# An ffn gain moved into the gather's copies, one more down chunk loaded ahead, and a start without the wait for constants

## The reference

```
h = _rms_norm(x, norm_mix[l]);  z = h @ w_in[l]
... three attentions of z, concatenated to mix ...
x = x + mix @ w_out[l]
x = x + _hier_moe(_rms_norm(x, norm_ffn[l]), w_group[l], b_group[l], w_expert[l], ...)
```

```
h = jax.nn.silu(xb @ w_gate[e]) * (xb @ w_up[e])
return h @ w_down[e]
```

## Time and profile before

| | |
|---|---|
| median of 3 runs | 1176.25 us (1175.04 to 1177.41) |
| the profiled execution | 1173.85 us, of which its span is 1171.9 us |
| PE busy | 930.9 us, 79% of the span |
| PE weight loads | 582.0 us, 50% |
| DVE busy | 335.0 us, 29% |
| ACT busy | 195.2 us, 17% |
| HBM read | 443.57 MB, 379 GB/s over the span |
| mean granted PE clock | 0.906 of full speed |

### The profile page before, as it was taken

One profiled execution on the slowest core, in us unless ns is written; L12 is line 12 of the kernel. 1 busy time (PEld: TensorE's weight loads), 2 busy tenths in 40 slices (PEclk: granted clock), 3 DMA queues, 4 the chain that ended last, 5 costly groups with the idle time before them and its releaser, 6 DMA issues.

```text
span 1171.9 us, 23254 instructions
## 1 busy us (share of the span) xinstructions
PE 930.9 (79%) x10294; PEld 582.0 (50%) x10299; DVE 335.0 (29%) x978; ACT 195.2 (17%) x527; POOL 18.7 (2%) x38
## 2 busy tenths in 40 slices
PE   8999999767567766775899999997776677557765
PEld 5876666434334433543478766664343434234433
DVE  3656552211111111111137465521111111111112
ACT  2234321001000100110112442211010001001002
POOL 1000000000000000000010001000000000000000
PEclk9999999989888888888999999999887888788878
DMA  7956499999999999999998256999999999999995
GB/s 308 404 237 258 200 379 423 435 428 428 427 433 426 429 426 435 425 429 427 401 386 322 80 218 270 382 429 430 427 430 427 429 426 431 428 430 427 428 424 245
DMA packets 34455, 446.16 MB, mean 381 GB/s; under 512 B 9648, under 2 KB 11056, under 8 KB 14256
## 3 DMA queue, kind: packets, MB, share of 16 engines
q1 hardware_dynamic: 33792, 444.54, 90.3%
q10 hardware_dynamic: 560, 0.09, 0.0%
HBM read 443.57 MB, written 1.05 MB: 379 GB/s over the span
## 4 chain that ended last, share of the span: by engine, by line
DMA 50%; PE 45%; issue 2%; DVE 1%; ACT 1%; another core or an unknown queue 0%; SPq 0%; ACTq 0%; POOLq 0%; POOL 0%; DVEq 0%
DMA ring<-in_w_down 18%; DMA arena<-in_gate_up 14%; DMA xb<-in_w_down 14%; PE pv L1751 10%; PE pj L1374 8%; PE tr L1776 5%; DMA ring<-in_gate_up 3%; PE pj L1380 2%; PE tr L1735 2%; PE pj L1486 2%; PE pj L1786 2%; PE pj L1606 2%; PE pj L1581 1%; PE pj L1615 1%; PE lg L1404 1%
## 5 line engine op out<-in xcount | busy, mean ns | idle before, releaser
L1751 PE MATMUL pv<-ring,xT 128*32 128x256 f32 x3072 | 228.5, 458 | 110.8 <-DMA ring<-in_gate_up 110.8
L1751 PEld LDWEIGHTS pv<-ring,xT 128*32 128x32 f32 x3072 | 110.2, 127 | 218.0 <-DMA ring<-in_gate_up 109.8
L1222 DVE TENSOR_SCALAR arena<-arena 128x128 f32<-128x128 f32 x64 | 14.5, 227 | 667.2 <-ACT arena L806 666.9
L1751 PE MATMUL pv<-arena,xT 128*32 128x256 f32 x1024 | 85.5, 500 | 67.1 <-DMA arena<-in_gate_up 67.1
L642 ACT ACTIVATE arena<-pv 128x256 f32<-128x256 f32 x64 | 24.6, 384 | 513.3 <-PE pv L1751 513.3
L1374 PE MATMUL pj<-xT,ring 128*128 128x256 f32 x448 | 100.2, 381 | 0.0
L1776 PE MATMUL tr<-ring,arena 128*32 128x256 f32 x1360 | 81.9, 380 | 16.5 <-issue 10.1
L1751 PEld LDWEIGHTS pv<-arena,xT 128*32 128x32 f32 x1024 | 38.7, 139 | 112.6 <-DMA arena<-in_gate_up 73.4
L1374 PEld LDWEIGHTS pj<-xT,ring 128*128 128x128 f32 x448 | 84.3, 190 | 12.9 <-issue 1.1
L1786 PE MATMUL pj<-arena 32*128 32x256 f32 x512 | 72.5, 400 | 6.7 <-ACT arena L642 6.7
L1786 PE MATMUL lg<-arena 32*128 32x256 f32 x512 | 72.5, 401 | 0.0
(11 more groups left out here) (237 smaller groups left out, 856.8 us busy)
## 6 DMA issues: line engine op xcount, KB each, us to landing
ring<-in_gate_up SPq DMA_DIRECT2D x42, 4096.0 KB, 48.5
ring<-in_w_down SPq DMA_DIRECT2D x38, 2048.0 KB, 41.4
arena<-in_gate_up SPq DMA_DIRECT2D x14, 4096.0 KB, 41.9
xb<-in_w_down SPq DMA_DIRECT2D x18, 2048.0 KB, 40.8
ring<-in_w_in_chunks SPq DMA_DIRECT2D x10, 2048.0 KB, 21.3
ring<-in_gate_up SPq DMA_DIRECT2D x10, 2048.0 KB, 8.2
ring<-in_w_out_halves SPq DMA_DIRECT2D x4, 2048.0 KB, 33.2
arena<-in_gate_up SPq DMA_DIRECT2D x4, 2048.0 KB, 49.4
```

Source lines behind the costliest of these rows:

```text
L1751: ins = mm(gu_ps[i * CAP:(i + 1) * CAP, :], xg[:, j, c:c + CAP], w, start=(j == 0), stop=(j == KD - 1), tile_position=(0, i * CAP), skip_g ...
```

## The change

There are three edits.

1. The weight of the ffn norm leaves `rows`. `rows` is now x times rms, copied by ACT straight from x. The weight is the per-partition scale of the copies out of the gather, for a feature lies on one partition there. A scale is one number for each partition, so one copy serves one block of 128 columns: a gather has eight copies of 128 where it had two of 512, and `gate_up` waits for each block ahead of its step. `weight`, `gain_ffn`, its two 512 KB loads and the semaphore `x_weighted` are gone.
2. The memory and the place in SP's list that `gain_ffn` had now serve the fourth chunk of down 3. The load of that chunk behind `d_used[0]` is gone.
3. PE's and DVE's waits for `consts_in` move behind the first products: DVE waits ahead of the first `diag`, PE in `spread_rms`.

```diff
-D_LOADS = {1: 2, 2: 2}
+D_LOADS = {1: 2, 2: 2, GU_PLACES - 1: 0}
...
                 sp.wait_ge(lg_done, at(l, NS, 8))
-                sp.dma_start(gain_ffn, bcast_row(norm_ffn, l, D_MODEL)).then_inc(gain_f_in, 16)
+                sp.dma_start(spare[3], down[SPLIT][:, 3]).then_inc(spare_full[3], 16)
...
                 sp.wait_ge(sums_open, l + 1)
-                sp.wait_ge(x_weighted, at(l, TOK, TOK))
+                sp.wait_ge(rows_ready, at(l, 2 * TOK, 2 * TOK))
...
-                        elif kind == "d" and e >= SPLIT:
+                        elif kind == "d" and e > SPLIT:
...
-                                ks = slice(len(spare) if e == SPLIT else 0, KE)
-                                sp.dma_start(d_place[i][:, ks], rows_of[:, ks]).then_inc(d_full[i], 16)
+                                sp.dma_start(d_place[i], rows_of).then_inc(d_full[i], 16)
...
-            act.dma_start(gain_R, ffn_blocks_d.rearrange("p (l j) -> p l j", l=DEPTH)).then_inc(gain_r_in, 16)
+            act.dma_start(gains, ffn_blocks_d.rearrange("p (u l j) -> p u l j", u=2, l=DEPTH)).then_inc(gain_r_in, 16)
...
-                    act.wait_ge(x_weighted, at(l, TOK, t + 1))
+                    act.wait_ge(x_added, at(l, PARTS, (2, PARTS)[t]))
...
-                             weighted[:, 512 * half:512 * half + 512].rearrange("q (p j) -> q p j", j=KD),
+                             x[:, t, 512 * half:512 * half + 512].rearrange("q (p j) -> q p j", j=KD),
...
                     def gathered(q):
 
-                        for half in range(2):
-                            act.wait_ge(wide_done, at(r, WIDE, gather_use(q) + half))
-                            copy(xg[:, 4 * half:4 * half + 4, :].rearrange("p j s -> p (j s)"), tr[:, half]).then_inc(wide_read, 1)
+                        for j in range(KD):
+                            if j % 4 == 0:
+                                act.wait_ge(wide_done, at(r, WIDE, gather_use(q) + j // 4))
+                            copy(xg[:, j, :], wide_ps[:, j * P:(j + 1) * P], scale=gain_G[:, l, j:j + 1]).then_inc(wide_read, 1)
...
-            dve.wait_ge(consts_in, 16)
 
             for l in range(DEPTH):
...
+                dve.wait_ge(consts_in, 16)
                 for t in range(TOK):
...
-                dve.wait_ge(ssq_ready, rbase + 6)
-                weight(0, 0, D_MODEL).then_inc(x_weighted, 1)
...
-                dve.wait_ge(rows_ready, at(l, 2 * TOK, 2))
-                own.mark(weight(1, 512, D_MODEL))
...
-                weight(1, 0, 512).then_inc(x_weighted, 1)
...
-                if l == 0:
-                    pe.wait_ge(consts_in, 16)
-
...
                 def spread_rms():
 
+                    pe.wait_ge(consts_in, 16)
                     pe.wait_ge(more_consts_in, 16)
...
-                        if j == KD // 2 and other_half:
-                            pe.wait_ge(wide_read, other_half)
+                        if gathered is not None:
+                            pe.wait_ge(wide_read, gathered + j)
```

More of the change, by code:

```diff
@@ L314, in trunk @@
         h_rows = take(HALF)
-        y = take(D_MODEL)[:, 0:D_MODEL // QUAD]
+        y = take(D_MODEL // QUAD)
         xnT_up = zT_flat[:, 1024:2048].rearrange("p (t j s) -> p t j s", t=TOK, j=KD // 2)
@@ L326, in trunk @@
         cnt = take(N_EXPERTS)
-        flags = take(N_EXPERTS * MORE)
+        flags = lam_in.rearrange("p v d -> p (v d)")[:, 0:N_EXPERTS * MORE]
         codes = take(OVER)
-        assert taken[0] <= 2048 + D_MODEL
-        taken[0] = 2048 + D_MODEL
+        assert taken[0] <= 2048
+        taken[0] = 2048
         rlog = take(TOK * R_COLS).rearrange("p (t n) -> p t n", t=TOK)
@@ L363, in trunk @@
         over_free = sem("over_free")
-        x_weighted, sums_open, rows_ready = sem("x_weighted"), sem("sums_open"), sem("rows_ready")
+        sums_open, rows_ready = sem("sums_open"), sem("rows_ready")
         sums_zeroed, upper_spent, upper_in = sem("sums_zeroed"), sem("upper_spent"), sem("upper_in")
@@ L717, in _ @@
                 square_sums(l)
+                act.wait_ge(gain_r_in, 16)
                 for t in range(TOK):
@@ L843, in _ @@
                                 act.wait_ge(o_wide, i * 2 + 1)
-                                copy(xg[:, :, 0:CAP], wide_ps[:, 0:KD * CAP].rearrange("p (j s) -> p j s", j=KD)
-                                     ).then_inc(o_wide_read, 1)
+                                for j in range(KD):
+                                    ins = copy(xg[:, j, 0:CAP], wide_ps[:, j * CAP:(j + 1) * CAP], scale=gain_G[:, l, j:j + 1])
+                                ins.then_inc(o_wide_read, 1)
                                 act.wait_ge(o_gu, i + 1)
@@ L1739, in gather, with gate_up @@
                     return last
-                def gate_up(both, c, other_half=0, signal=False, in_pieces=False):
+                def gate_up(both, c, gathered=None, signal=False, in_pieces=False):
                     for j in range(KD):
@@ L1806, in down_landed @@
                             pe.wait_ge(d_full[n % D_PLACES], d_loads(l, n))
-                        steps = [d_place[n % D_PLACES][:, k] for k in range(KE)]
                         if n == SPLIT:
@@ L1810, in down_landed @@
                                 pe.wait_ge(part_in, 16 * (l + 1))
-                            return [*spare, *steps[len(spare):]]
-                        return steps
+                            return spare
+                        return [d_place[n % D_PLACES][:, k] for k in range(KE)]
                     def tokens(q):
@@ L1914 @@
 WIDE = 2 * 2 + BODY
+READS = 2 * KD + BODY
 PAIRS = 4
@@ L1970 @@
     arrays["const_table"] = layer_constants()
-    arrays["ffn_blocks"] = np.ascontiguousarray(
-        given["norm_ffn"].reshape(DEPTH, KD, P).transpose(2, 0, 1).reshape(P, DEPTH * KD))
+    blocks = given["norm_ffn"].reshape(DEPTH, KD, P).transpose(2, 0, 1).reshape(P, DEPTH * KD)
+    steps = given["norm_ffn"].reshape(DEPTH, P, KD).transpose(1, 0, 2).reshape(P, DEPTH * KD)
+    arrays["ffn_blocks"] = np.concatenate([blocks, steps], 1)
     arrays["x_turned"] = np.ascontiguousarray(given["x"].reshape(TOK, P, P, KD).transpose(0, 2, 3, 1).reshape(TOK, P, D_MODEL))
```

31 lines of the change are left out of this document (15 added, 16 removed).

## The result

The changed kernel takes 1168.62 us (median of 5 runs, 1168.1 to 1170.0). The kernel before took 1175.04 us beside it (5 runs, 1174.32 to 1177.41). The ratio is 0.9947, with a 95% interval of 0.9934 to 0.996. That is 6.2 us less, 4.7 to 7.8. The forecast was 1171.0 us, 5.2 us less than before.

What follows compares the result with a forecast made beforehand. The prediction took the expert load stream at 429 GB/s as the bound. Bytes 2.44, SP's list 2.28 and the start 0.5 make 5.2 us, off the median of 1176.25: 1171.0 us, range 1168.5 to 1174.5.

Steps and rivals of the forecast that it cites:

- What bounds the kernel: Expert stages: the stream of weight loads at 429 GB/s sets the time; PE's speed matters only ahead of that.
- Bytes: Expert load stream: 512 KB of down 3 leaves it in each layer, 1.22 us a layer, 2.44 us in both.
- SP's list: Gate/up 5's load goes out 2.0 us sooner without the wait for expert 0, closing a dip; 2.28 us, range 0 to 4.2.
- the hole behind 170 us: Load rate of 335 and 279 GB/s for four microseconds early in each layer's experts; loss 0.88 and 1.40 us.
- The start: Kernel's beginning: first products start between 6.0 and 6.3 us without the wait for constants; about 0.5 us gained, once.
- DVE's multiplications at 0: Attention part: three multiplications a layer go, but the release is tied with one that stays; nothing gained.
- the copies at 0: Gather: eight ACT copies of 128 columns replace two of 512; no product step waits, so no cost.
- no second dry spot: Later load issues in the expert stage: 6.9 us of queue left at down 4's issue, above the 4.4 that was enough.
- Bytes and start alone: Rival: the dip is not the short queue's or the earlier issue doesn't close it; 1173.3 us, chance 0.18.
- The stream gives it back: Rival: a later wait for a place, or an end other than bytes, leaves the start alone; 1175.7 us, chance 0.12.
- slower: Rival: gather copies hold up expert 0's products and the loads behind; 1180.9 us at 1.0 us a copy, chance 0.07.
- All of the landings' gap: Rival: the dip is worth 4.2 us in both layers, by load landings; 1169.1 us, chance 0.06.

Runs made afterwards that it cites:

- E9: Changed kernel with one 512 KB chunk cut from the loads of down 8, 14, 20 and 26 in each layer, part of the computation left out; 1159.47 us.
- E13: Changed kernel with the fourth chunk cut from the loads of down 4 to 7 in each layer, part of the computation left out; 1159.91 us.
- E10: Changed kernel with the down loads of experts 6, 8 ... 28 each issued as two, 24 more loads, same bytes; 1173.01 us.
- E4: Changed kernel with down 3's fourth chunk back in the stream, but issued behind gate/up 5; 1173.29 us, ratio 0.9985 to the kernel before.
- E12: Changed kernel with a 32 KB load of down 3's fourth chunk added behind gate/up 5 and the wait for expert 0; 1169.22 us.
- E2: Changed kernel with down 3's fourth chunk back in the stream ahead of gate/up 5, as before; 1174.72 us, ratio 1.0002 to the kernel before.
- E3: Changed kernel with the chunk still early, but SP again waiting for expert 0's down product ahead of gate/up 5; 1170.03 us.
- E14: Changed kernel with the down loads of experts 4 to 7 each issued as two, 8 more loads, same bytes; 1171.04 us.
- E1: Kernel before with the third edit alone, the later waits for the constants; 1173.6 us, ratio 0.9993.
- the kernels of the table: The kernel before, the changed kernel, E1, E2, E3 and E4, compared by time, rate and landing of gate/up 6; 1168.62 to 1175.04 us.
- like kernels: Kernels expected to run alike: the kernel before with E1 and E2, stretches averaging 848.7 us; the changed kernel with E8, E11 and E12, 843.9 us.
- E8: Changed kernel with two unscaled copies of 512 columns a gather as before, the second norm's weight left out; 1169.99 us.
- E11: Changed kernel with the turn of the three down places moved on, so down 4 goes to place 0 and is issued sooner; 1169.19 us.
- E6: Changed kernel with each copy of a block out of the gather split in four of 32 columns; 1173.94 us.

## Why the prediction came out right, step by step

**What bounds the kernel: right.** 4 MB taken out gave 8.2 to 9.2 us wherever they stood (E9, E13), and 12 splits a layer lowered the rate and cost as much as that rate says (E10).

**Bytes: right in kind, too small.** The prediction had 2.44 us. The runs put 3.4 to 4.9 us on the chunk, the landings 3.7, the stretches 2.9 to 4.0. The step that failed is "524288 B over 429 GB/s": that is the price of a chunk inside a longer load. This one stood by itself in a stream whose queue was short, and besides its bytes it made or deepened a hole in the rate (E4 against E12, E2 against E3). Being a load of its own accounts for 0.15 to 0.3 us of it a layer, if the price of E10 and E14 holds here.

**SP's list: right in kind, too large.** The prediction had 2.28 us for the hole behind 170 us, all of it due to gate/up 5's later issue. The hole is gone, and by the rates it was worth 1.8 to 2.9 us, so its size was read rightly. But the earlier issue alone gives 1.8 us by the landings, 0.9 to 1.9 by the stretches and 0.5 to 2.0 us by the times. The rest of the hole goes with the chunk. The failed step is to give the whole dip to one of two causes that stood 0.4 us apart in the list; "chunk in the queue" and "gate/up 5 late" were never told apart before E3 and E4. The upper bound, 4.2 us by the landings, rested on one pair of landings in layer 0, 2.1 us too far apart. Layer 1 of before has 13.2 us between the same two, but the kernels with the same loads and order have 12.7 in both layers (E1) and 12.1 and 11.6 (E2), against the 11.0 of the bytes. In after that gap is gone: gate/up 5 lands 167.17 + 15.2 - 172.6 = 9.8 us behind L503's load, and 4.19 MB at 429 GB/s are 9.8 us. But over both layers and the kernels of the table the gain at gate/up 6 is 38.1 - 35.3 = 2.8 us a layer, of which 1.22 are bytes. That leaves 1.6 us for all of the hole, 3.2 in both, between the forecast's value and its upper bound.

**The two errors offset each other.** 2.44 + 2.28 = 4.7 us were forecast for both parts, and the landings show 5.5, the windows with the bytes 4.2 to 5.3, the stretches 4.9. The forecast of "each expert stage some 2.3 us shorter" has 2.3 and 2.6 us against it by the means of like kernels (3.4 and 2.3 in after itself). That the sum came out is in part luck: the change took away the chunk and the late issue at once. A change that took only one of them, as E3 or E4 does, would have been forecast wrongly by about 1 us or more, and both of these were.

**The start: 0.5 us forecast, 0.14 found in after.** The products start sooner, by 0.42 us in after and by nearly nothing (6.78 against 6.82) in five of the other kernels with this edit. What "is late next" was looked for at `spread_rms`; PE's own matmuls on zeros and the landing of `w_in`'s second half come before it. Then DVE's pause of 0.36 us ahead of 150.20 takes most of what is left. L496's issue was at 155.84 before, at 155.49 in E1, and between 155.63 and 156.45 in all kernels with the changed DVE program. E1 gave 0.8 us with an interval from 2.1 down to none, which cannot tell. "From there PE is busy nearly without a gap" was the weak sentence: there is DVE in the chain, and its own program had changed.

**DVE's multiplications at 0, the copies at 0, no second dry spot, 429 GB/s unchanged: right**, by after's rows, E8 and E11. E2 has the multiplications, the copies and the start as the changed kernel has them and comes out at 1.0002, and layer 1's attention part takes 155.06 us before and 155.05 after. The copies were even cheaper than forecast, since eight back to back overlap.

**Rivals.** "Bytes and start alone" falls with E3 and E4, which differ from after and E2 by the order, though the times alone don't say so clearly (E2 and E4 have intervals that touch); the landings and stretches do. "The stream gives it back" and "slower" fall with the result. "All of the landings' gap" forecast 1169.1 us, nearer to the median than the forecast itself. The hole was worth 1.8 to 2.9 us by the rates and 3.2 by the landings, but not 4.2, and not all of it by the earlier issue, as this rival had it.

**Still open.** Why 512 KB behind or ahead of a 4 MB load make a hole, when 32 KB at the same place or more bytes in a full queue do not. Why PE's pace and DVE's pause in the first layer fall as they do. The difference of 0.7 to 1.3 us between the changed kernel's own runs and the 4.9 to 5.5 us that traces and like kernels show is within the spread, and may be nothing.

## What to carry to other kernels

When a stream of loads is the bound, price an edit in two parts: its bytes over the stream's rate, and the holes near the place where it stands, counted from the same event in both layers and not in fixed windows. Take more than one length of window and more than one kernel, since a single ruler here read the same hole as 1.8 or 2.9 us. Where two suspects stand side by side in an issue list, move each alone before giving either the whole hole. A gain at the start counts only if every engine in the chain to the stream passes it on; look at the last issue ahead of the stream and not at the first instruction.

## What the runs showed of the hardware

Scaled copies of psum on ACT, which take 0.37 us each with 128 columns and 0.40 us with 32, follow one another in 0.27 us with 128 columns (after) and in 0.18 us with 32 (E6). POOL's instruction for `rms` behind the last square sum takes 0.56 us in after, and took 0.84 us in before, where DVE's multiplication of 512 columns ran beside it; beside the one of 1024 columns the same kind of instruction took 1.49 us (136.14 and 716.20 in before). Each time it ended 0.4 us behind the end of DVE's instruction. A pause of some 0.35 us stood at different places of DVE's first layer in the two programs, and at neither place in the second layer. A further load in a full queue costs 0.15 to 0.18 us by E10's time, though no row shows an engine waiting for its issue.
